# The heads stage of an attention encoder kernel, rebuilt: where its transposes stand, what is turned, and how much one store carries

## The reference

```python
q = (rmsnorm(q_lat, qlat_g) @ w_uq).reshape(B, S, MLA_HEADS, QK_HEAD)
q = rmsnorm(q, q_norm_g)
q = jnp.concatenate([q[..., :QK_NOPE], apply_rope(q[..., QK_NOPE:], cos, sin)], axis=-1)
kv = (rmsnorm(kv_lat, kvlat_g) @ w_ukv).reshape(B, S, MLA_HEADS, QK_NOPE + V_HEAD)
k_nope, v = kv[..., :QK_NOPE], kv[..., QK_NOPE:]
k = rmsnorm(jnp.concatenate([k_nope, k_pe_h], axis=-1), k_norm_g)
k = jnp.concatenate([k[..., :QK_NOPE], apply_rope(k[..., QK_NOPE:], cos, sin)], axis=-1)
return block_attention(q, k, v, QK_HEAD ** -0.5)
```

## Time and profile before

| | |
|---|---|
| median of three executions | 3777.64 us |
| profiled execution: its time | 3780.94 us |
| profiled execution: its span in the trace | 3779.2 us |
| PE busy in the span | 3386.3 us (90%) |
| stage `heads` | 214 to 596 us |
| mean rate of all DMAs over the span | 142 GB/s |

### The profile page before, as it was taken

How to read it: one execution, slowest core, us unless ns; L and a number is a source line. 1 busy time by engine, 2 the same in 40 slices (tenths; PEclk the granted TensorE clock), 3 DMA queues, 4 the chain that set the end, 5 groups by cost and what they waited for, 6 DMA issues and landing times. The chain is left out here.

```text
span 3779.2 us, 49146 instructions
## 1 busy us (share of the span) xinstructions
PE 3386.3 (90%) x16168; PEld 2772.4 (73%) x16168; DVE 2048.4 (54%) x3037; ACT 1599.4 (42%) x2396; POOL 1336.9 (35%) x885
## 2 busy tenths in 40 slices
PE   8957776999999999999769799897999977899899
PEld 8956664777676767777549688786788867878787
DVE  4455656888787888888537533212333336622211
ACT  4434443777676767777535322101222224422100
POOL 1124443888787888888531000000000011100000
PEclk9988887999999999999889799998999988889999
DMA  7757775222122221222434599655322234398554
GB/s 282 256 200 222 208 226 137 51 51 51 37 51 50 51 52 37 51 52 57 93 140 161 151 282 270 217 196 178 131 88 100 88 139 179 106 287 235 168 199 167
DMA packets 456334, 538.17 MB, mean 142 GB/s; under 512 B 54744, under 2 KB 371544, under 8 KB 436432
## 3 DMA queue, kind: packets, MB, share of 16 engines
q1 hardware_dynamic: 456144, 535.81, 46.4%
HBM read 324.98 MB, written 210.61 MB: 142 GB/s over the span
## 5 line engine op out<-in xcount | busy, mean ns | idle before, releaser
L1174 POOL TENSOR_TENSOR at_acc<-at_acc,at_ph 128x1024 f32<-128x1024 f32 x288 | 690.7, 2398 | 83.7 <-ACT at_ph L1100 69.6
L1208 DVE TENSOR_TENSOR at_pl<-at_sc,at_ph 128x1024 fp32r<-128x1024 f32 x408 | 498.4, 1222 | 190.4 <-ACT at_sc L1101 166.2
L1100 ACT ACTIVATE at_ph<-at_sc 128x1024 fp32r<-128x1024 f32 x408 | 419.1, 1027 | 405.9 <-PE at_sc L1020 405.2
L1194 DVE TENSOR_REDUCE at_mx<-at_mxp 128x1 f32<-128x512 f32 x816 | 522.5, 682 | 32.5 <-PE at_mxp L1031 30.3
L1101 ACT ACTIVATE at_sc<-at_sc 128x1024 f32<-128x1024 f32 x408 | 416.3, 1020 | 0.0
L1016 PE MATMUL at_sc<-at_qt,at_kt 97*128 97x512 f32 x816 | 337.0, 413 | 63.2 <-DMA at_qt<-at_neg 31.4
L1018 PE MATMUL at_sc<-at_qt,at_kt 96*128 96x512 f32 x816 | 330.1, 405 | 0.0
L1020 PE MATMUL at_sc<-at_qt,at_kt 96*128 96x512 f32 x816 | 329.1, 403 | 0.0
L1045 PE MATMUL at_o_hi<-at_ph,at_v 128*128 128x512 f32 x816 | 325.0, 398 | 1.5 <-DVE at_half L1213 1.5
L1047 PE MATMUL at_o_lo<-at_pl,at_v 128*97 128x512 f32 x816 | 323.4, 396 | 0.0
L1031 PE MATMUL at_mxp<-at_kt,at_qt 96*128 96x512 f32 x816 | 280.2, 415 | 27.4 <-DMA at_kt<-kT 20.8
(11 more groups left out here) (245 smaller groups left out, 7476.2 us busy)
## 6 DMA issues: line engine op xcount, KB each, us to landing
ma_h<-hT SPq DMA_DIRECT2D x40, 1024.0 KB, 4.9
ogT<-ga_st SPq DMA_DIRECT2D x160, 256.0 KB, 3.5
ou_o<-ogT SPq DMA_DIRECT2D x40, 1024.0 KB, 6.1
ga_h<-hT SPq DMA_DIRECT2D x64, 512.0 KB, 7.3
hT<-lat_n_h SPq DMA_DIRECT2D x24, 1024.0 KB, 6.2
hT<-sg_n_h SPq DMA_DIRECT2D x24, 1024.0 KB, 3.8
qT<-hd_st SPq DMA_DIRECT2D x60, 384.0 KB, 6.7
kT<-hd_st SPq DMA_DIRECT2D x60, 384.0 KB, 5.9
```

Source lines behind the costliest of these rows:

```text
L1100: act.activation(ph[:, g], sc[g % 2][:], ACT.Exp, scale=SCALE).then_inc(p_hi, 1)
L1174: pool.tensor_tensor(acc[:, c.slot, :], f32(ph[:, (g - 1) % 4]).rearrange("p b n -> p (b n)") if t == 1 else acc[:, c.slot, :], now, ALU.a ...
L1194: dve.tensor_reduce(mx[:, n:n + 1], mxp[n % 2][:], AX.X, ALU.max).then_inc(mx_in, 1)
L1208: dve.tensor_tensor(pl[:, g], sc[g % 2][:], f32(ph[:, g]), ALU.subtract).then_inc(p_lo, 1)
```

## The change

It rebuilds the stage `heads`:

- The transposes of a tile are spread over two later steps. The keys of tile t-2 are turned in three groups between the three groups of query matmuls of tile t, the queries of tile t-1 in three groups between the three groups of key and value matmuls of tile t.
- Keys are turned in full blocks: the 1152 numbers of a token are taken as nine blocks of 128, three blocks in a group, instead of twelve heads of 96. The keys' gains are multiplied into the queries' (`gcol` is now the product of both), so that a turned key needs no scale. The lo half of a turned key is a plain subtraction. `kT` becomes `[2, 1152, tokens]`; attention loads its heads from there in rows of the same length as before.
- ACT and DVE begin a step with the keys and values of the tile before: squares, `ks`, values' hi half; mean, values' lo half. The turned keys follow, then the queries.
- `stq` and `stk` hold a pair of tiles (256 tokens). Three query stores of 768 KB and six key stores of 384 KB, in rows of 1024 bytes, go out once per pair. Each has one buffer.
- POOL makes the tables ahead of the first tile in place of DVE (nine operations) and the rotated part of the keys (`key_rope`).
- The squares of queries and keys have tiles of their own (`sqq`, `sqk`). The loop is `run_tiles`: four steps written out, a loop over six pairs, then six steps (two of them only empty the pipeline).

`Tile(j, u, by)` names the tile `by` places away, with `n` its number, `slot` its parity and `half` its pair; `after` waits unless the value is known to be 0 or less. The core of the diff:

```diff
-                            if u == 1:
-                                turn(j, 0, first, 2 * c + k)
-                            elif not first:
-                                turn(j - 1, 1, False, 2 * c + k)
+                def turn_k(t, c):
+                    if c == 0:
+                        pe.wait_ge(k_sc, t.n + 1)
+                        pe.wait_ge(k_rope, t.n + 1)
+                    if c < 2:
+                        pe.wait_ge(q_lo, t.n * G + (c + 2))
+                    else:
+                        pe.wait_ge(k_lo, t.n * G + 1)
+                    flat = kn[:, t.slot].rearrange("p h n -> p (h n)")
+                    for n in range(KB):
+                        b = c * KB + n
+                        m = pe.transpose(pt[c % 2][:, n, :], flat[:, b * P:(b + 1) * P], K.ident[:])
+                    m.then_inc(k_turned, 1)
...
+                def turn_q(t, c):
+                    if c == 0:
+                        pe.wait_ge(q_rope, t.n + 1)
+                    if c < 2:
+                        after(pe, k_lo, t.n * G + (c - 1))
+                    else:
+                        pe.wait_ge(q_lo, t.n * G + 1)
                     for n in range(HPG):
-                        m = pe.transpose(pt[c % 2][0:QK, n, :], src[:, u, (c % G) * HPG + n, :],
-                                         K.ident[:])
-                    m.then_inc(turned, 1)
+                        m = pe.transpose(pt[1 - c % 2][0:QK, n, :], qn[:, t.slot, c * HPG + n, :], K.ident[:])
+                    m.then_inc(q_turned, 1)
```

The new step of PE:

```diff
+                def step(j, u):
+                    queries(Tile(j, u), Tile(j, u, -2))
+                    keys_values(Tile(j, u), Tile(j, u, -1))
```

The new step of ACT:

```diff
+                def step(j, u):
+                    t, t1, t2 = Tile(j, u), Tile(j, u, -1), Tile(j, u, -2)
+                    if t1.within(TILES):
+                        key_square(t1)
+                        key_out(t1)
+                        value_hi(t1)
+                    if t2.within(TILES):
+                        for c in range(G):
+                            copy_k(t2, c)
+                    if t.within(TILES):
+                        query_square(t)
+                    if t1.within(TILES):
+                        copy_q(t1, 0)
+                    if t.within(TILES):
+                        query_out(t)
+                    if t1.within(TILES):
+                        copy_q(t1, 1)
+                        copy_q(t1, 2)
```

The new step of DVE:

```diff
+                def step(j, u):
+                    if t1.within(TILES):
+                        key_mean(t1)
+                        value_lo(t1)
+                    if t2.within(TILES):
+                        for c in range(G):
+                            low_k(t2, c)
+                    if t.within(TILES):
+                        query_mean(t)
+                    if t1.within(TILES):
+                        low_q(t1, 0)
+                        key_scale(t1)
+                        low_q(t1, 1)
+                    if t.within(TILES):
+                        query_scale(t)
+                    if t1.within(TILES):
+                        low_q(t1, 2)
```

The copy of a turned group of keys on ACT (that of queries waits for `q_st` alike):

```diff
+                def copy_k(t, c):
+                    act.wait_ge(k_turned, t.n * G + (c + 1))
+                    if t.slot == 0:
+                        after(act, k_st[c], t.half * 32)
+                    act.copy(stk[:, c, 0, :, t.slot * P:(t.slot + 1) * P], pt[c % 2][:, 0:KB]).then_inc(k_hi, 1)
```

The new step of SP:

```diff
+                def step(j, u):
+                    if t1.within(TILES):
+                        store_v(t1)
+                    if t2.within(TILES) and t2.slot == 1:
+                        for c in range(G):
+                            store_k(t2, c)
+                    if Tile(j, u, 2).within(TILES):
+                        sp.wait_ge(kv_mm, t.n + 1)
+                        load_lat(Tile(j, u, 2))
+                    if t1.within(TILES) and t1.slot == 1:
+                        for c in range(G):
+                            store_q(t1, c)
```

The new step of POOL:

```diff
+                def step(j, u):
+                    query_root(t)
+                    query_rope(t)
+                    key_root(t)
+                    key_rope(t)
```

More of the change, by code:

```diff
@@ L561, in _ @@
+                run_tiles(sp, DRAIN, step)
                 for u in range(2):
-                    sp.wait_ge(v_out[u], 16 * NP)
-                for c in range(2 * G):
-                    sp.wait_ge(t_out[c], 16 * TILES)
+                    sp.wait_ge(v_out[u], 16 * TILES // 2)
+                for c in range(G):
+                    sp.wait_ge(q_st[c], 16 * TILES // 2)
+                    sp.wait_ge(k_st[c], 32 * TILES // 2)
             @block.tensor
             def _(pe):
[L568 to L575, removed]
-                    for n in range(HPG):
-                        m = pe.transpose(pt[c % 2][0:QK, n, :], src[:, u, (c % G) * HPG + n, :],
-                                         K.ident[:])
-                    m.then_inc(turned, 1)
@@ L620, in _ @@
                 w.round_hi(act)
[L621 to L644, removed]
+                def copy_q(t, c):
+                    act.wait_ge(q_turned, t.n * G + (c + 1))
+                    if t.known and t.n == 0:
+                        act.wait_ge(gains, 17)
+                    if t.slot == 0:
+                        after(act, q_st[c], t.half * 16)
+                    act.activation(stq[:, c, :, 0, t.slot * P:(t.slot + 1) * P], pt[1 - c % 2][0:QK], ACT.Copy,
+                                   scale=gcol[:, 0:1]).then_inc(q_hi, 1)
@@ L645, in step, with key_out, query_square @@
+                def key_out(t):
+                    after(act, k_sc, t.n)
+                    act.copy(ks[:], kv[:, :, 0:NOPE]).then_inc(k_out, 1)
+                def query_square(t):
+                    act.wait_ge(q_mm, t.n + 1)
+                    after(act, q_red, t.n)
+                    act.activation(sqq[:].rearrange("p (g n) -> p g n", g=G), pq[:, :, 0:HPG * QK],
                                    ACT.Square, scale=float(QK) ** -0.5).then_inc(q_sq, 1)
-                    copies(j, u, first, range(G))
@@ L647, in step, with query_out @@
-                    if not (first and u == 0):
-                        act.wait_ge(q_sc, i)
+                def query_out(t):
+                    after(act, q_sc, t.n)
                     act.copy(qs[:].rearrange("p (g h) n -> p g (h n)", g=G),
                              pq[:, :, 0:HPG * QK]).then_inc(q_out, 1)
[L651 to L654, removed]
@@ L775, in _, with query_scale @@
-                run_pairs(dve, NP, step)
-                for c in range(2 * G):
-                    low_t(NP - 1, 1, c)
+                def query_scale(t):
+                    dve.wait_ge(q_rstd, t.n + 1)
+                    after(dve, q_turned, (t.n - 1) * G)
+                    dve.wait_ge(q_out, t.n + 1)
+                    dve.tensor_tensor(qn[:, t.slot], qs[:], rstd[:, 0, :].rearrange("p (h o) -> p h o", o=1)
+                                      .broadcast_to([P, NH, QK]), ALU.mult).then_inc(q_sc, 1)
@@ L781 @@
+                run_tiles(dve, DRAIN, step)
 class Chunk:
```

343 lines of the change are left out of this document (178 added, 165 removed).

## The result

Four executions of the changed kernel took 3687.48 to 3694.51 us, median 3690.18. Four of the kernel before beside them took 3774.42 to 3778.50, median 3777.15. The ratio is 0.9772 (95% interval 0.9755 to 0.9789): 87 us faster. I had said 104 us faster, 3673 us, so the sign and the mechanism came out and 17 us of the gain did not.

The account below looks back on a forecast made before the run. Heads was taken as bound by a chain through DVE and POOL, not an engine. Step 1 at 250.8, steps 2 to 19 215.6, drain 25.4 us end it at 491.8, not 596.2: 104.4 us gained, 3673 us, range 3655 to 3710.

Parts of the forecast that it names:

- What bound the kernel before: In heads, PE waits for the values' lo half behind a DVE and POOL chain: 18 waits, 50.5 us, low clock behind.
- The step of 11.34 us: PE's work per tile after the change: query and key/value matmuls plus query and key transposes sum to 11.34 us.
- The hand-written chain: One step written out across PE, ACT, DVE and POOL; `pt[0]`, by way of query scaling, has 0.6 us of slack.
- The wait for single buffers: ACT stands 1.9 to 2.1 us at even steps' third key group; PE loses 1.1 us there, 0.3 in odd steps.
- The rate of 1024-byte rows: Turned stores in heads: 51.4 ns per 1024-byte row, 319 GB/s; ends are 277 and 364 GB/s.
- the line's 319: GB/s for 1024-byte rows from the straight line through measured 512-byte (277 GB/s) and 6144-byte (364 GB/s) rows.
- the rule's 301: GB/s for 1024-byte rows by the Trainium skill's three fixed cycles plus bytes/32 per packet, from the measured 277.
- Keys in full blocks: Nine key transposes at 0.12 us, 1.07 us on PE; ACT's copies 0.687 to 0.49 us; DVE's three lo halves plain subtractions.
- The ends: Heads' start and drain: step 1 ends at 250.8 us; the drain takes 25.4 us, to 491.8.
- A longer row is not cheaper: Rival: stores stay at 277 GB/s, ACT stands 4.2 us, a pair takes 26.4 us; 3696 us, chance 0.14.
- A little cheaper: Rival: 1024-byte rows at 301 GB/s, ACT stands 2.9 us, a pair takes 25.1 us; 3683 us, chance 0.10.
- The chain stays the bound: Rival: crossings in DVE's chain cost 0.1 to 0.2 us more, clock falls, step near 14 us; 3709 us, chance 0.15.

Follow-up runs that it names:

- The moved scaling: Changed kernel with VectorE's keys' scaling moved behind the queries' scaling; stage 305.8 us against 301.2, queries' root 2.267 us.
- the doubled one: Changed kernel with the scaling of the keys' plain part done twice, writing the same values; stage 300.1 us against 301.2, root 3.58 us.
- two buffers and the other order: Changed kernel with two buffers for turned keys and two query stores issued ahead of the latents' load; 3673.19 us, ratio 0.9733 to the kernel before.

## Why the prediction was right, and where it was off

**What bound the kernel before: right.** PE waited for the values' half behind a chain through DVE and POOL, and the clock fell behind the wait. Moving that one operation in the kernel before gives 66.7 us and lifts the clock from 0.89 to 0.98.

**The step of 11.34 us: mis-sized, and here most of the lost gain lies.** I took the queries' root at 2.277 us and had 0.6 us in hand. It takes 3.60 us, so the chain through `pt[0]` should become the bound by 3.60 - 2.28 - 0.6 = 0.7 us: 12.05 us. The undisturbed step is 12.0. Over 18 steps that is 18 x 0.66 = 11.9 us. The hand-written chain was thus good within 0.1 us and one duration in it was wrong. That duration came from a row in which nothing of that kind ran beside the operation. The wait stands where the chain has it: PE stands for DVE's first key lo half ahead of the third key group in all 18 steps, 11.7 us in all. The Trainium skill says in "GPSIMD Engine Reference", section "Specifications", that POOL's interfaces to SBUF are shared with VectorE and that there is contention with DVE instructions that have two SBUF inputs. The moved scaling agrees on where it strikes; the doubled one shows that it isn't a price per operation. PE's own sum was nearly right: 11.2 us where I had 11.34.

**The wait for single buffers: right in kind, too small.** Steps 2 to 19 took 235.1 us (step 1 ended at 252.65, step 19 at 487.7, the drain took the other 27.4). Less 18 x 12.0 that leaves 19.1 us for waits on stores where I had 8 x 1.1 + 9 x 0.3 = 11.5. Two things were off. I had left out the waits for query stores, 13.3 us in 8 waits. And for keys I had ACT stand 1.9 to 2.1 us in an even step, at the third group alone; it stood 33.5 us in eight even steps, 4.2 in the mean and up to 5.6, mostly spread over the three groups. I had the last key store land 19.9 us behind `kv_mm`; in the step shown above `kv_mm` came at 289.1 and ACT got the third buffer back at 312.2, 23 us behind. Why the stores took that much longer stays open. The single waits stayed under the 4 us that I had named as a sign of being wrong (the longest was 3.4), their sum in a step did not in those five: here the forecast had the kind of wait and not its size. With two buffers and the other order, steps 2 to 19 take 215.5 us, 18 x 11.97, and the drain 27.1: the 19.6 us that go are these waits.

**The rate of 1024-byte rows: nearly right.** A pair moves 7.60 MB; at 327 GB/s 23.2 us, of which the 2.88 MB of long rows take 7.9, so 4.72 MB take 15.3 us: 308 GB/s, between the line's 319 and the rule's 301, which is the nearer. The same sum with 512-byte rows gives 264 GB/s, where 277 was read from the earlier trace rows. DMA share and rate in the steady part, 0.90 and 292, are below the 0.95 and 310 of the forecast, for the steps are longer.

**Keys in full blocks: sized as work of PE, ACT and DVE, and there of little weight.** That turning them by head instead costs 30 us, most of it in the waits for stores, I had not seen.

**The ends.** Step 1 ended 1.8 us later than said, the drain took 27.4 instead of 25.4 (whose terms add up to 25.1). The stage: 1.8 + 11.9 + 7.6 + 2.0 = 23.3 us longer than forecast, 515.1 against 491.8. In the profiled pair 12.7 us came back outside the stage (93.5 - 80.8), 9.2 of them in attention, which I take for variation. Without that the profiled time would have missed by 23 us and not by 11: that the total came nearer than the stage is luck. The range to 3710 would still have held it.

**The rivals.** "A longer row is not cheaper" is nearest in number: 3696 us, and the stage's end at 515 where it came at 515.1. That is chance, for its reason did not come true: the rows ran at 308 GB/s and not at 277. "A little cheaper" (3683, rate 301) is nearest in the rate, but the rate explains few of the 23 us. "The chain stays the bound" was right as to what bounds the undisturbed step, at 12.0 us and not 14, and by one long operation rather than many crossings. The sign that I had named for it, a wait of PE for DVE at the third key group in every step, came true. The clock didn't fall with it.

## What to carry to other kernels

Look first for the one operation at the end of an in-order engine's list that frees the bottleneck's buffer: moving it gave four fifths of what a rebuilt stage gave. When a step is written out by hand, ask of every duration what ran beside it when it was measured and what will run beside it now, POOL beside two-operand operations of DVE above all. When stores carry more and stand in one queue, count the single buffer's turnaround for every kind of store and for every buffer of it, and put ahead of a waiting load those that are ready.

## What the runs showed that I had not expected

- A POOL operation on 12 numbers a partition grew from 2.28 to 3.60 us under one DVE operation with two SBUF operands, and stayed at 3.58 under two in a row. The root had begun first each time, and DVE's operations inside it took 0.94 to 0.96 us. One of 384 numbers grew from 1.01 to 1.59 under the same operation. What in the chip makes this a price paid once was not found.
- With row length, bytes and count of stores equal, turning keys by head and storing them from 96 partitions costs the stage 29.8 us, some 5 of them for the engines' added work. Why the stores are slower stays open.
- The attention stage, with code that differs in its load addresses alone, differs by up to 10 us between the profiles of different kernels, and by 1.8 and 3.1 between two of the same kernel. A difference of a few microseconds in one stage can be read only in that stage, and there only above some 3 us.
